# Quadrant turns through HBM, and two more seven-product groups a quarter, in the MLP of a hybrid block

## What is computed

```
h2 = rms_norm(x, norm_ffn_g)
u = square(relu(h2 @ w_up))       # w_up   (2048, 8192)
x = x + u @ w_down                # w_down (8192, 2048)
return rms_norm(x, norm_final_g)
```

## Time and profile before

| | |
|---|---|
| median of the runs | 1476.49 us |
| the profiled execution | 1476.18 us, span 1474.4 us |
| PE busy | 1465.7 us, 99% |
| DVE busy | 1190.9 us, 81% |
| ACT busy | 766.8 us, 52% |
| DMA | 299.33 MB, mean 203 GB/s |
| granted TensorE clock | 0.999 of full speed |

### The profile page before, as it was taken

How to read it: one execution, slowest core, us unless ns; L and a number is a source line. 1 busy time by engine, 2 the same in 40 slices (tenths; PEclk the granted TensorE clock), 3 DMA queues, 4 the chain that set the end, 5 groups by cost and what they waited for, 6 DMA issues and landing times.

```text
span 1474.4 us, 18772 instructions
## 1 busy us (share of the span) xinstructions
PE 1465.7 (99%) x6968; PEld 1279.8 (87%) x6968; DVE 1190.9 (81%) x1558; ACT 766.8 (52%) x986; POOL 15.0 (1%) x21
## 2 busy tenths in 40 slices
PE   9999999999999999999999999999999999999997
PEld 8888888888888888888888888888888888888886
DVE  7977887776577788777799988888897888889877
ACT  7656565444455555444445555555554555555553
POOL 0000000000000000000000000000000000000000
PEclk9999999999999999999999999999999999999999
DMA  9556544667655566556765665656666656655563
GB/s 333 191 169 211 184 154 164 229 203 241 213 180 184 186 199 206 194 200 200 248 233 181 202 219 201 218 185 207 217 204 202 208 199 226 214 199 193 198 209 114
DMA packets 149801, 299.33 MB, mean 203 GB/s; under 512 B 5232, under 2 KB 5360, under 8 KB 149488
## 3 DMA queue, kind: packets, MB, share of 16 engines
q1 hardware_dynamic: 149168, 297.51, 59.9%
q10 hardware_dynamic: 576, 1.06, 0.2%
HBM read 296.45 MB, written 2.10 MB: 202 GB/s over the span
## 4 chain that ended last, share of the span: by engine, by line
PE 98%; issue 1%; DVE 1%; POOLq 0%; POOL 0%; DVEq 0%; ACT 0%
PE acc L545 88%; PE acc L827 3%; PE banks L776 3%; PE acc L776 1%; PE banks L564 1%; PE banks L583 1%; PE banks L573 0%; PE banks L591 0%; DVE ta_lo L1775 0%; PE banks L680 0%; PE banks L696 0%; PE banks L695 0%; PE banks L693 0%; PE acc L603 0%; DVE final L1787 0%
## 5 line engine op out<-in xcount | busy, mean ns | idle before, releaser
L865 ACT ACTIVATE whi<-raw 128x1024 fp32r<-128x1024 f32 x542 | 569.2, 1056 | 577.3 <-PE acc L545 517.9
L1222 DVE TENSOR_TENSOR wlo<-raw,whi 128x1024 fp32r<-128x1024 f32 x542 | 655.1, 1223 | 213.1 <-ACT whi L865 208.5
L545 PE MATMUL acc<-whi,ta_hi 128*128 128x512 f32 x1308 | 497.4, 380 | 0.0
L545 PE MATMUL acc<-wlo,ta_hi 128*128 128x512 f32 x1308 | 495.7, 379 | 0.0
L545 PE MATMUL acc<-whi,ta_lo 128*128 128x512 f32 x1308 | 495.7, 379 | 0.0
L545 PEld LDWEIGHTS acc<-whi,ta_hi 128*128 128x128 f32 x1308 | 247.2, 189 | 36.7 <-issue 1.2
L545 PEld LDWEIGHTS acc<-whi,ta_lo 128*128 128x128 f32 x1308 | 247.2, 189 | 35.1
L545 PEld LDWEIGHTS acc<-wlo,ta_hi 128*128 128x128 f32 x1308 | 247.3, 189 | 34.5
L545 PE MATMUL acc<-whi,tb_hi 128*128 128x512 f32 x560 | 212.3, 379 | 0.0
L545 PE MATMUL acc<-wlo,tb_hi 128*128 128x512 f32 x560 | 212.2, 379 | 0.0
L545 PE MATMUL acc<-whi,tb_lo 128*128 128x512 f32 x560 | 212.2, 379 | 0.0
(11 more groups left out here) (208 smaller groups left out, 1049.2 us busy)
## 6 DMA issues: line engine op xcount, KB each, us to landing
raw<-in_w_in SPq DMA_DIRECT2D x64, 1024.0 KB, 5.2
raw<-in_w_up SPq DMA_DIRECT2D x64, 1024.0 KB, 5.3
raw<-in_w_down SPq DMA_DIRECT2D x57, 1024.0 KB, 5.0
raw<-in_w_gate SPq DMA_DIRECT2D x32, 1024.0 KB, 5.3
raw<-in_w_att SPq DMA_DIRECT2D x16, 1024.0 KB, 5.0
raw<-in_w_ret SPq DMA_DIRECT2D x16, 1024.0 KB, 5.0
raw<-in_w_out SPq DMA_DIRECT2D x16, 1024.0 KB, 5.0
raw<-in_w_down SPq DMA_DIRECT2D x14, 512.0 KB, 4.3
```

Of the source, the lines that this page charges most:

```text
L545: last = nc.tensor.matmul(paired(acc[B.parity][:, t, :]), a[:, k, tok], halves_in_turn(b), start=(k == 0 and n == 0), stop=(k == (B.ends + ...
L865: nc.scalar.activation(whi[:, B.ring_at(u), :], raw[:, B.raw_at(u), :], ACT.Copy).then_inc(hi_ready, 1)
L1222: V_.tensor_tensor(wlo[:, at, :], raw[:, B.raw_at(u), :], whi[:, at, :].bitcast(f32), ALU.subtract).then_inc(lo_ready, 1)
```

## The change

*The turn.* In the MLP, DVE now makes four transposes of 128x256 for a block (`turn_in_quads`) in place of 16 of 32x256: each 32x32 piece is turned on its own partitions, into `buf[3]`. ACT then stores the 512 KB to a buffer `parking` in HBM by one DMA (`park`), waits for it (`parked`), and brings the pieces to their partitions by four loads of 128 KB into `buf[1]` (`fetch`, `fetch_next`). The halves of `tb` are made from there, in the block after. Up block 2's values are fetched a second time at the start of the next quarter, since their combinations are needed then. Operations are no longer turned and split in turn: the four transposes lie together after a block's fourth unit.

*The groups.* Quarters 1 to 3 have three late groups, in up blocks 0, 2 and 3: columns 0 and 1 with the last four chunks as before, columns 0 and 1 with the four chunks before those, and columns 2 and 3 with those. A late group lies ahead of the last two units of its up block. The down blocks d0, d1, J and K of quarters 0 to 2 have 4 plain units each where they had 6; those of quarter 3 keep theirs. T2 has a place of its own (`sum_two`), and there are two sets of `mixed_hi`, `mixed_lo`. `gfin` is loaded at the end of the MLP's loads, not ahead of them.

```diff
-TOP = KCH - 2 * UCH
 SUMS, MIXED, PRODUCTS = 3, 4, 3
-FOLDS = (5, 7)
+BOUNDARY_FOLDS, LATE_FOLDS = 5, 7
+BOUNDARY = (2, 3, 3)
+LATE = {0:(0,1,3),2:(0,1,2),3:(2,3,2)}
+EVERY = True
+AGAIN = any(c == GROUPS - 2 for _, _, c in LATE.values())
+GROUPS_OF_QUARTER = EVERY + len(LATE)
+FOLDS_OF_QUARTER = BOUNDARY_FOLDS * EVERY + LATE_FOLDS * len(LATE)
+MIXES_OF_QUARTER = 1 + AGAIN
+TURNS_OF_QUARTER = GROUPS + AGAIN
...
+        left_out = [sum(UCH for j, k, _ in LATE.values() if c in (j, k)) for c in range(GROUPS)]
+        standing = EVERY or last
+        before = 0 if first else -2 * UCH * len(LATE)
+        self.up, self.late = [], []
+        for i in range(GROUPS):
+            hosted = i in LATE and not first
+            E = Block(B6 + i, 8, q, before)
+            self.late.append(None)
+            if hosted:
+                n = list(LATE).index(i)
+                mixed = (q - 1) * MIXES_OF_QUARTER + (1 if LATE[i][2] == GROUPS - 1 else 2)
+                self.late[i] = Group(E, UNITS - 2, q * GROUPS_OF_QUARTER - (len(LATE) - n),
+                                     q * FOLDS_OF_QUARTER - LATE_FOLDS * (len(LATE) - n), mixed, LATE[i], False)
+                before += 2 * UCH
...
+    def of_down(self, left_out, standing):
+        return [UNITS - n - (UCH if standing and c in BOUNDARY[:2] else 0) for c, n in enumerate(left_out)]
...
+        sum_two = place("sum_two", [P, UCH, COLS], f32, at_f + 8 * K)
+        mixed_his = [place(f"mixed_hi{n}", [P, MIXED, UCH, P], f32r, at) for n, at in enumerate((at_f, at_c + 24 * K))]
...
+            def load_up(Q, q, i):
+                (E, tail), G = Q.up[i], Q.late[i]
+                col = q * D + i * COLS
+                load_rows(E, w_up, col, 0, range(3))
+                if G:
+                    load_left(G, q * D - D)
+                    load_right(G, q * D - D)
+                load_rows(tail, w_up, col, 0, range(3, 4))
...
+                        gemm(E, ta_hi, ta_lo, 0, 6)
+                        if G:
+                            seven_products(G)
+                        gemm(tail, ta_hi, ta_lo, 6, 8)
+                pe.wait_ge(t_free, q * 4 + (T_STAGE6 + 2))
+                gemm(Q.down[0], tb_hi, tb_lo, 0, 4)
...
+                gemm(Q.J, tb_hi, tb_lo, 0, Q.units[2])
+                if Q.boundary:
                     pe.wait_ge(t_free, q * 4 + (T_STAGE6 + 4))
-                seven_products(boundary_group(q, B[6]), B[6], B[7])
+                    seven_products(Q.boundary, Q.J, Q.K)
...
+                for i in range(1 if first else 0, GROUPS):
+                    (E, tail), G = Q.up[i], Q.late[i]
+                    split(E, 0, 2)
+                    if i > 1:
+                        hi_from_exchanged(Q.turn(q, i - 1), i - 2)
+                    split(E, 2, 4)
+                    if i:
+                        if first and i == 1:
+                            act.wait_ge(rstd2_ready, 1)
+                        else:
+                            act.wait_ge(quads_turned, q * 4 + (i - 1))
+                        if Q.late[i - 1]:
+                            act.wait_ge(sum_lo_ready, Q.late[i - 1].halves(3))
+                        squared_relu(Q.up[i - 1][1])
+                    if AGAIN and not first and i == 1:
+                        mixed_hi_of(GROUPS - 2, (q - 1) * MIXES_OF_QUARTER + 1)
+                    if G:
+                        split_for_seven(G, E, 4, parks=(q * 4 + i, i - 1) if i else None)
+                        split(tail, 6, 7)
                     else:
-                        act.wait_ge(t_full, q * 4 + (T_STAGE6 + i - 1))
-                    squared_relu(B[i - 1])
-                    split(B[i], 4, B[i].ends + 1)
-                    if i == 4 and not last:
-                        split(B[5], 0, 2)
-                    hi_from_turned(q * 4 + (T_STAGE6 + i - 1), tb_hi, i - 1)
+                        split(E, 4, 5)
+                        if i:
+                            park(q * 4 + i, i - 1)
+                        split(E, 5, 7)
+                    if i:
+                        fetch_next(Q, q, i, first)
+                    split(tail, 7, 8)
...
+                    split(Q.down[1], 0, 1)
+                    park(q * 4 + 4, 3)
+                    split(Q.down[1], 1, 2)
+                fetch_next(Q, q, 4, first)
...
+                    split(Q.down[1], 2, 4)
+                    split(Q.J, 0, 1)
+                    hi_from_exchanged(Q.turn(q, 4), 3)
+                    split(Q.J, 1, 2)
+                    mixed_hi_of(GROUPS - 1, q * MIXES_OF_QUARTER)
...
+            def park(n, g):
+                act.wait_ge(quads_turned, n)
+                act.dma_start(parking[g], in_quads.rearrange("p o n -> p (o n)")).then_inc(parked, 16)
+            def fetch(g, n):
+                for o in range(QUADS):
+                    act.dma_start(exchanged_at[o * SQ:(o + 1) * SQ].rearrange("f i a n -> f i (a n)"),
+                                  parking[g].rearrange("(i f) (o n) -> o f i n", f=SQ, o=QUADS)[o]).then_inc(exchanged, 16)
+            def fetch_next(Q, q, i, first):
+                act.wait_ge(parked, (q * 4 + i) * 16)
+                if i > 1:
+                    act.wait_ge(t_free, q * 4 + (T_STAGE6 + i - 1))
...
+            def split_for_seven(G, B, begin, squares_of=None, parks=None):
+                u = G.at
+                split(B, begin, u - 1)
+                if parks:
+                    park(*parks)
                 if squares_of:
-                    residual_squares(squares_of, 1, down_sq)
-                sums_hi(G, 0)
-                sums_hi(G, 1)
-                split(B, 5, 6)
-                sums_hi(G, 2)
-                split(B, 6, 9)
+                    residual_squares(squares_of, 1, down_sq, buf[1])
+                sums_hi(G, 0, 1)
+                sums_hi(G, 1, 2)
+                split(B, u - 1, u)
+                sums_hi(G, 2, 3)
+                split(B, u, u + 3)
                 act.wait_ge(sum_set, G.sums(SUMS + 1))
-                split(B, 9, 10)
-
-            def sums_hi(G, m):
-                act.wait_ge(sum_set, G.sums(m + 1))
-                nc.scalar.activation(sum_hi[:, m], w_sums[m], ACT.Copy).then_inc(sum_hi_ready, 1)
+                split(B, u + 3, u + 4)
...
-                    turn_among(B[i], q * 4 + (T_STAGE6 + i - 1), buf[0][:], u_ready, q * 4 + i, ((4, 0, 10), (5, 10, 14)))
-                    short = i == 4 and not last
-                    rest = (lambda n: split(B[5], n, n + 1)) if short else (lambda n: split(B[i], 6 + n, 7 + n))
-                    rest(0)
-                    lo_from_turned(q * 4 + (12 + i), tb_hi, tb_lo, i - 1)
-                    rest(1)
...
+                Q = Quarter(q, first, last)
+                for i in range(1 if first else 0, GROUPS):
+                    (E, tail), G = Q.up[i], Q.late[i]
+                    if i == 0:
+                        split(E, 0, 3)
+                        add_residual(Q.last_down, 3)
+                        split(E, 3, 4)
+                    else:
+                        split(E, 0, 2)
+                        if i == 1 and AGAIN and not first:
+                            mixed_tokens(Q.turn(q, 0), (q - 1) * MIXES_OF_QUARTER + 1)
+                        if i > 1:
+                            lo_from_exchanged(q * 4 + (12 + i - 1), i - 2)
+                        split(E, 2, 4)
+                        turn_in_quads(q * 4 + i)
+                        if i == 1 and AGAIN and not first:
+                            mixed_lo_of(GROUPS - 2, (q - 1) * MIXES_OF_QUARTER + 1)
+                    if G:
+                        if i:
+                            dve.wait_ge(quads_turned, q * 4 + i)
+                        sums_for_seven(G, (q - 1) * MIXES_OF_QUARTER + (2 if AGAIN and i else 1))
+                        fold_in_passing(G, tail)
+                        split(tail, 7, 8)
+                    else:
+                        split(E, 4, 8)
...
+                split(Q.down[1], 0, 3)
+                if not last:
+                    add_residual(Q.down_end[0], 0)
+                split(Q.down[1], 3, 4)
+                if not wide:
+                    split(Q.J, 0, 1)
+                mixed_tokens(Q.turn(q, 4), q * MIXES_OF_QUARTER)
+                lo_from_exchanged(q * 4 + 16, 3)
...
+                ready = min(3, G.at - 2) if G else 3
+                split(Q.J, done, ready)
+                add_residual(Q.down_end[1], 1)
+                if G:
+                    split(Q.J, ready, G.at - 2)
+                    sums_for_seven(G, G.mixed)
...
+            def turn_in_quads(n):
+                dve.wait_ge(u_ready, n)
+                if later(n - 1):
+                    dve.wait_ge(parked, (n - 1) * 16)
+                for o in range(QUADS):
+                    piece = V_.transpose(in_quads[:, o, :].rearrange("p (m t n) -> p m t n", t=TILES, n=SQ),
+                                         by_chunk(buf[0][:])[:, :, :, o * SQ:(o + 1) * SQ])
```

(45 more changed lines are left out.)

371 lines of the change are left out of this document (206 added, 165 removed).

## The result

The changed kernel takes 1506.86 us (median of 4 runs, 1505.49 to 1507.4), the kernel before 1476.55 on the same chip: ratio 1.0204, 95% interval 1.0191 to 1.0217. The sign was forecast, the size was not: 1491.4 was forecast, within 1479 to 1503. The profiled execution took 1506.97 us, with a span of 1505.2 and a mean granted clock of 0.996.

The account below looks back on a forecast made before the run. PE was taken to bound the kernel, with DVE locally full and 1.0 us spare. 1476.18 - 7.8 (matmuls) + 10.6 (hosted blocks) + 12.4 (short boundaries) = 1491.4 us; range 1479 to 1503, 8 in 10.

Parts of the forecast that it names:

- The matmuls: PE, 13 seven-product groups instead of 7: six fewer matmuls per added group at 0.216 us, 7.8 us less.
- The chain on DVE from T1 to the fold: DVE in a group: T1's start to the first fold's end takes 14.45 us.
- DVE's due time: In a group, the first fold must end before PE's third product S2·T2; the kernel before had 1.0 us spare.
- Hosted blocks 2 and 3: Six up blocks with T1 behind the turn: PE waits 1.76 us in each, 10.6 us in all.
- The short boundaries: Boundary groups of quarters 0 to 2, J with four units: PE waits 2.83 us plus 1.3 each, 12.4 us.
- the timeline of the exchange: Store and four loads in the short down blocks: at 4.3 us a transfer, T1 is 1.3 us late on top.
- Block 0 has no turn ahead of its sums and keeps its old timetable: nothing.: Up block 0 of quarters 1 to 3: DVE's timetable stays, so PE waits nothing there.
- The last quarter keeps six units: nothing.: The last quarter's boundary group: its down blocks keep six units, so no wait is added.
- The transposes: Four 128x256 transposes per turn on DVE, ahead of T1 in hosted blocks: 0.447 us each, 1.79 us.
- rival of a slow exchange: Both transfers take 6.8 us, T1 4.5 late in each boundary: 1501 to 1505 us, chance 14%.
- averages: Rival: DVE's total work fits the quarter, local crowding is hidden, only the matmuls count: 1468.4 us, chance 12%.
- Transposes by the partition: Rival: transpose cost grows with partitions, 5.4 us more in nine places: about 1540 us, chance 4%.

Follow-up runs that it names:

- e5: The changed kernel with DVE's order in groups altered: one unit ahead of T1's low half, the first fold ahead of T3's low half; 1499.37 us, 1.0154.
- e11: e12 with e5's DVE order, d1's residual behind the first fold, one split behind the second fold and the other behind the third; 1486.56 us, 1.0066.
- e15: e14 with the second down block's residual ahead of the first sum again in the boundaries of quarters 0 to 2; 1474.07 us, 0.9983.
- e12: The changed kernel with the edits of e3, e4 and e9's last quarter together; 1496.67 us, 1.0133.
- e14: Ten groups (e2's table) in e13's DVE order, with the edits of e3 and e9's last quarter, loop kept; 1477.38 us, 1.0006.
- e9: The kernel before with only the turn through HBM, its seven groups kept, and the last quarter's first two J units made early; 1476.55 us, 1.000.
- e3: The changed kernel with up block 2's second fetch moved from the quarter's start behind all but the last of block 0's units; 1502.12 us, 1.0174.
- e2: The changed kernel with one more late group per quarter instead of two (blocks 0 and 2), J and K with six plain units; 1487.43 us, 1.0075.
- e4: The changed kernel with quarters 1 and 2 written out instead of looped; 1502.86 us, 1.0178.
- e1: The kernel before with only the turn through HBM, its seven groups kept and no second fetch; 1480.4 us, 1.0028.
- e13: e12 with a mixed DVE order in blocks 2, 3 and short boundaries: one split ahead of the second fold, one behind the third; 1482.46 us, 1.0038.
- e10: e11 with the loop over quarters 1 and 2 kept; 1489.12 us, 1.0086.

## Why the prediction was wrong, by its steps

*Right.* The matmuls (36 fewer, spacing 0.216). The chain on DVE from T1 to the fold (14.44 against 14.45), and with it that DVE's due time decides and not its average: e5, e11 and e15 (against the changed kernel, e12 and e14) moved nothing but this order and a few operations beside it and changed PE's waits as the due times say. Hosted blocks 2 and 3 lost 12.0 against 10.6; the excess is in block 3, where T1 also waits for corner loads, which I hadn't listed. The short boundaries lost 11.9 against 12.4; the timeline of the exchange with 4.3 us a store held there (4.3 to 4.5; in quarter 1 T1 came 2.3 us after J's start, forecast 2.5), and e12 shows the loss following the store one for one. `gfin` delayed nothing. The exchange in up blocks cost nothing (e9).

*Failed: "Block 0 has no turn ahead of its sums and keeps its old timetable: nothing."* It lost 10.9 us. I had looked at DVE's order alone. Its timetable hangs on the corner loads, and those met the second fetch and a K shortened by two units (2.92 us of wait at T1, where 1.0 was to spare): e3 takes the fetch away and the loss of quarters 1 and 3 goes. With K at six units the early fetch costs nothing (e2), so it takes both. In quarter 2 the jump back of the loop came on top: e4 turns 7.8 into 1.5. That the loop makes the stops is shown by e4; that they are the fetching of instructions is not. For it are the packet counts (between 1112 and 1290 none in e2, whose jump stops nothing, nine in the changed kernel); e4 has six there and no stop.

*Failed: "The last quarter keeps six units: nothing."* It lost 3.3 us. The number of units was kept, but not their order: the ends of d0 and d1 were put ahead of J's first units and d0's residual, which waits for PE, ahead of all of them. e1 and e9 show this step alone, 1480.4 against 1476.55.

*Off in size, and hidden by luck.* The transposes: I took 0.447 each, they are spaced 0.35, and the 0.25 us by which T1 waits for the last of them, which wasn't in the sum, made up for most of that. The restart: after each wait PE's first matmul takes 0.48 where the others take 0.38 (0.45 in a few places), and the next starts 0.32 later and not 0.22. The count has 2.9 us of this in all, but only what stands behind a place's last wait adds to the time, about 1.2 us for 12 waits for the fold, since the fold's end doesn't move with what PE lost ahead of it. And the price of a transfer: with the failed steps removed, the store takes 5.9 to 6.2 us in two of three boundaries, part of the way to my rival of a slow exchange (6.8). The forecast's own timeline, with a store 1.9 us longer, gives 4.1 + 1.9 = 6.0 us for such a boundary, and e12 lost 5.8 and 5.5: the mechanism holds, the 4.3 us doesn't. e12 lies 5.3 us above my forecast by its median, 6.6 by its profiled execution, in which the short boundaries lost 2.6 us more than I had summed and blocks 2 and 3 3.2 more. So a forecast without the two failed steps would have been too low too.

The rivals: averages didn't decide, in the form as changed. Transposes by the partition are excluded: `L1880` takes 0.41 us at 128 partitions, spaced 0.35. The Trainium skill (Vector Engine (DVE) Microarchitecture Reference, 3.8 The reshape front-end and per-opcode configuration) has a 32x32 reorder array in front of each bank of 32 channels, which sustains one element per cycle per lane; that the partitions are then free, as I took from it, agrees with the run. The estimate of 3.2 us for 512 KB, worked out from the figures that the Trainium skill (DMA: Bandwidth & Descriptors, Anatomy of one DMA) fits to DMAs of the software path, was too low here: the store's median was 4.6 us in the changed kernel, and 4.1 to 6.1 in the others.

Open is what slows the store in some boundaries, and whether a form with 13 groups can be made to pay; e13 still lacks 6 us.

## What to carry to other kernels

A saved matmul is worth 0.216 us only if every due time beside it still holds: for each place that the change touches, and for the places just before and behind, write down each wait of the bound engine, the chain that must end there, and the loads that this chain starts with. "Nothing changes here" is a claim to be priced like the others: the order of units, the issue time of the loads, the size of a loop's body. And when one due time is moved, compute the next one too before the next is run.

## What of the hardware was not expected

- A loop's jump back can stop PE. The changed kernel's cost two stops of 3.5 and 2.5 us between starts, and the granted clock was 0.50 for 6.8 us, from 0.8 us after the first stop on. In e3 the same jump (0.9 and 2.9 us between starts) left no half clock; what decides that isn't shown.
- A wait costs up to 0.1 us more than itself on PE: behind it the second matmul starts 0.29 to 0.32 us after the first, not 0.22, even after a wait of 0.20 us (e10).
- The same 512 KB store, at the same place of the program, took from 3.8 to 6.3 us in four kernels until the loads behind it could be issued; a corner load issued 7.6 us ahead of T1 held it up for 2.9 us, where one issued 4.8 ahead of it before the change didn't.
- Four 128x256 transposes took 1.42 us, ten of 32x256 4.47: per transpose no more for four times the partitions.
